# Two transformer blocks, the fp32 down projections: residual kept in SBUF, weight blocks in a ring of four instead of eight

## What is computed

```python
x = x + rms_norm(mix @ w_out[l], post_mix_norm[l])
h = rms_norm(x, pre_ffn_norm[l])
u = causal_dwconv(h @ w_up[l], conv_w[l], conv_b[l])
gate, up = jnp.split(u, 2, axis=-1)
y = (jax.nn.gelu(gate, approximate=True) * up) @ w_down[l]
x = x + rms_norm(y, post_ffn_norm[l])
```

## Time and profile before

| | |
|---|---|
| median of the runs | 2494.13 us (2492.53 to 2497.15) |
| profiled execution, its own time | 2492.89 us |
| its span | 2491.1 us |
| down1 in it, from the first raw block's issue to the last product | about 911.8 to 1155.8 us |
| down2 in it, likewise | about 2235.4 to 2480 us |

### The profile page before, as it was taken

The page is one execution under the profiler, slowest core; times in us unless marked ns, Lnnn a source line. Parts: engine busy times, 40 slices in busy tenths (PEclk is TensorE's granted clock), DMA queues, the critical chain, the costliest instruction groups (busy, mean ns, idle before and its releaser), DMA issues.

```text
span 2491.1 us, 38756 instructions
## 1 busy us (share of the span) xinstructions
PE 2474.5 (99%) x15321; PEld 2133.2 (86%) x15321; DVE 1820.7 (73%) x2218; ACT 1353.0 (54%) x1792; POOL 177.2 (7%) x82
## 2 busy tenths in 40 slices
PE   9999999999999999999999999999999999999998
PEld 9999988888888888888888888888888888888886
DVE  6665675777777779787495968775767777778887
ACT  6554564655555556555545454554555555555554
POOL 1000000030211300000000000000012121120000
PEclk9999999999999999999999999999999999999999
DMA  7765335655566565655655555545666555656664
GB/s 238 256 203 160 119 133 190 215 189 188 189 187 193 187 223 198 221 198 195 191 178 162 177 154 177 154 151 186 204 194 192 187 188 186 195 189 220 220 212 159
DMA packets 242886, 470.75 MB, mean 189 GB/s; under 512 B 14520, under 2 KB 24049, under 8 KB 241601
## 3 DMA queue, kind: packets, MB, share of 16 engines
q1 hardware_dynamic: 240513, 457.64, 56.9%
q0 software_dynamic: 2144, 11.30, 1.4%
q10 hardware_dynamic: 96, 0.02, 0.0%
HBM read 462.59 MB, written 6.32 MB: 188 GB/s over the span
## 4 chain that ended last, share of the span: by engine, by line
PE 96%; DVE 2%; ACT 1%; issue 1%; DMA 0%; SPq 0%; DVEq 0%; ACTq 0%
PE acc L330 13%; PE tp L330 13%; PE acc L310 7%; PE acc L311 7%; PE acc L312 7%; PE tp L332 7%; PE acc L332 7%; PE acc L613 3%; PE acc L612 3%; PE acc L614 3%; PE acc L1382 2%; PE acc L1385 2%; PE acc L1384 2%; PE tp L626 1%; PE tp L627 1%; PE tp L628 1%
## 5 line engine op out<-in xcount | busy, mean ns | idle before, releaser
L297 DVE TENSOR_TENSOR wlo<-raw,whi 128x1024 fp32r<-128x1024 f32 x679 | 847.7, 1256 | 489.3 <-ACT whi L292 487.8
L292 ACT ACTIVATE whi<-raw 128x1024 fp32r<-128x1024 f32 x679 | 716.9, 1059 | 777.4 <-PE acc L332 221.9
L330 PE MATMUL acc<-ahl,whi 128*128 128x512 f32 x1408 | 489.9, 392 | 0.6 <-DVE ahl L415 0.6
L330 PE MATMUL tp<-ahl,whi 128*128 128x512 f32 x1408 | 489.5, 391 | 0.0
L332 PE MATMUL tp<-ahl,wlo 128*128 128x256 f32 x1408 | 394.2, 280 | 0.0
L332 PE MATMUL acc<-ahl,wlo 128*128 128x256 f32 x1408 | 393.9, 280 | 0.0
L330 PEld LDWEIGHTS acc<-ahl,whi 128*128 128x128 f32 x1408 | 263.4, 187 | 58.8 <-issue 1.0
L330 PEld LDWEIGHTS tp<-ahl,whi 128*128 128x128 f32 x1408 | 263.3, 187 | 57.7
L310 PE MATMUL acc<-whi,ahl 128*128 128x512 f32 x752 | 298.7, 397 | 1.9 <-DVE ahl L2209 1.5
L312 PE MATMUL acc<-whi,ahl 128*128 128x512 f32 x752 | 293.0, 390 | 0.0
L311 PE MATMUL acc<-wlo,ahl 128*128 128x512 f32 x752 | 292.7, 389 | 0.0
(11 more groups left out here) (339 smaller groups left out, 3798.4 us busy)
## 6 DMA issues: line engine op xcount, KB each, us to landing
raw<-in_w_up_dram SPq DMA_DIRECT2D x176, 512.0 KB, 4.3
raw<-in_ffn_w_in_dram SPq DMA_DIRECT2D x176, 512.0 KB, 4.3
raw<-in_hgrn_w_in_dram SPq DMA_DIRECT2D x160, 512.0 KB, 3.6
raw<-in_w_in_dram SPq DMA_DIRECT2D x87, 512.0 KB, 3.6
raw<-in_w_down_dram SPq DMA_DIRECT2D x48, 512.0 KB, 5.0
raw<-in_ffn_w_out_dram SPq DMA_DIRECT2D x48, 512.0 KB, 5.2
more<-in_w_down_dram SPq DMA_DIRECT2D x40, 512.0 KB, 5.1
more<-in_ffn_w_out_dram SPq DMA_DIRECT2D x40, 512.0 KB, 4.9
```

Of the source, the lines that this page charges most:

```text
L292: act.activation(whi[:, s, :], raw[:, s, :], ACT.Copy).then_inc(hi_done, 1)
L297: dve.tensor_tensor(wlo[:, s, :], raw[:, s, :], whi[:, s, :].bitcast(F32), ALU.subtract).then_inc(lo_done, 1)
L330: pe.matmul(o[:, ct % 2, :].rearrange("p (a t) -> p a t", a=2), whi[:, s, c], ahl[:, :, kt, :], start=(kt == 0), stop=False, skip_group_ch ...
```

## The change

The residual x has memory of its own all the time (the memory on which `more` lay), `more` is gone, and all 88 blocks of a down projection go through the four places of `raw`. The store of x, the two reads of it and the waits that belong to them are gone.

```diff
-SLOTS = 2 * RING
-SLOT = [m % SLOTS if m < M_DOWN - SLOTS else m % RING for m in range(M_DOWN)]
+SLOT = [m % RING for m in range(M_DOWN)]
 TURN = [SLOT[:m].count(SLOT[m]) for m in range(M_DOWN)]
 BEFORE = [max([k for k in range(m) if SLOT[k] == SLOT[m]], default=None) for m in range(M_DOWN)]
-MAIN_TURNS, MORE_TURNS = SLOT.count(0), SLOT.count(RING)
-LAST_MORE = max(d.n for d in DOWN if d.m is not None and SLOT[d.m] >= RING)
+TURNS_DOWN = SLOT.count(0)
...
-        with ExitStack() as r:
-            x = sb("x", [P, NT, D], where=r)
-        more = sb("more", [P, RING, CK * GC])
+        x = sb("x", [P, NT, D])
...
         def down_slot(m):
 
-            return raw[:, SLOT[m], :] if SLOT[m] < RING else more[:, SLOT[m] - RING, :]
+            return raw[:, SLOT[m], :]
...
-                if m == M_DOWN - RING:
-                    x_back(sp, ph)
                 if m < RING:
                     sp.wait_ge(lo_done, cb[ph] - RING + m + 1)
-                elif m < SLOTS:
-                    sp.wait_ge(sem("x_out"), 16 * (DOWNS.index(ph) + 1))
                 elif BEFORE[m] in SECOND:
                     sp.wait_ge(sem("sums"), ub[ph] + SECOND[BEFORE[m]] + 2)
                 else:
                     sp.wait_ge(lo_done, cb[ph] + FREED[BEFORE[m]] + 1)
...
-        def x_away(pool, b, out_x):
-
-            pool.wait_ge(out_x, 2 * NG)
-            pool.dma_start(x_home(), x[:, :, :]).then_inc(sem("x_out"), 16)
-
-        def x_back(sp, ph):
-
-            sp.wait_ge(lo_done, cb[ph] + LAST_MORE + 1)
-            for t in range(NT):
-                sp.dma_start(x[:, t, :], x_home()[:, t, :]).then_inc(sem("x_back"), 16)
...
             def add(q, t):
                 c = slice(q * GC, (q + 1) * GC)
-                if ph in ub:
-                    dve.wait_ge(sem("x_back"), 16 * NT * (DOWNS.index(ph) + 1))
...
             pool.memset(prime[:, :], 0.0).then_inc(sem(f"{ph}_hid"), 1)
-            x_away(pool, b, out_x)
```

More of the change, by code:

```diff
@@ L260, in bass_two_blocks @@
         tp = [ctx.enter_context(nc.psum_tensor(f"tp{i}", [P, 4, S], F32)) for i in range(2)]
-        landed = [sem(f"landed{i}") for i in range(SLOTS)]
+        landed = [sem(f"landed{i}") for i in range(RING)]
         hi_done, lo_done, chunk_used = sem("hi_done"), sem("lo_done"), sem("chunk_used")
@@ L277, in bass_two_blocks @@
             g += groups
-            m += RING * MAIN_TURNS if name in ub else chunks
+            m += RING * TURNS_DOWN if name in ub else chunks
         def load(sp, n, s, src, kk=CK):
@@ L466, in down_slot @@
         def down_slot(m):
-            return raw[:, SLOT[m], :] if SLOT[m] < RING else more[:, SLOT[m] - RING, :]
+            return raw[:, SLOT[m], :]
         def down_landed(e, ph, m):
-            turns = rb[ph] // RING if SLOT[m] < RING else MORE_TURNS * DOWNS.index(ph)
-            e.wait_ge(landed[SLOT[m]], 16 * (turns + TURN[m] + 1))
+            e.wait_ge(landed[SLOT[m]], 16 * (rb[ph] // RING + TURN[m] + 1))
         def back_load(sp, ph, w):
@@ L491, in back_load @@
                              w_tile(w, CK * (2 * sg + r), i * (2 * GC) + c * GC)).then_inc(landed[SLOT[m]], 16)
-        def x_home():
-            return T["scratch"].rearrange("a p c -> (a p c)")[0:P * NT * D].rearrange("(p n c) -> p n c", p=P, n=NT)
-        def x_away(pool, b, out_x):
-            pool.wait_ge(out_x, 2 * NG)
-            pool.dma_start(x_home(), x[:, :, :]).then_inc(sem("x_out"), 16)
-        def x_back(sp, ph):
-            sp.wait_ge(lo_done, cb[ph] + LAST_MORE + 1)
-            for t in range(NT):
-                sp.dma_start(x[:, t, :], x_home()[:, t, :]).then_inc(sem("x_back"), 16)
         def last_products(pe, ph, k, n, xhi, xlo, kts):
```

## The result

The kernel after takes **2502.87 us**, the median of five runs (2501.91 to 2507.01), against 2492.61 us for the kernel before beside it: a ratio of 1.0035, 95% interval 1.0024 to 1.0047. The profiled executions differ by 10.0 us (spans 2501.1 and 2491.1). The forecast was 2505.3 us, +11.2.

The account below looks back on a forecast made before the run. PE was taken as the bound, busy 2474.5 of 2491.1 us, with loads hidden. Down1 +6.6, down2 +5.4, less 0.8 gained, gave +11.2 on 2494.1: 2505.3 us, range 2496 to 2515.

Parts of the forecast that it names:

- Places 1, 2 and 3: down1's first pair, summed groups at 19, 30, 41: PE 1.2, then 3.4, then 4.6 us late in all.
- The walk through DVE: First pair of down1: late block landings delay DVE's sums, L722 to 970.0, L719 to 989.2 and 1011.1.
- From DVE to PE: Summed steps: a PE step can begin 1.67 us after its low part begins on DVE.
- Place 3: Group at 41: step 44's earliest start 1021.2 against 1016.91, 4.3 us late, 4.7 with b22; 4.6 taken.
- Second pair: Three crossings into summed groups, a loop through b21's landing: 0.6, 0.7 and 0.7 us late, 2.0 us.
- down2: Second down phase: same timeline as down1, quicker landing at place 1 spares 1.2 us, so 5.4 us lost.
- The gain of the tail: Last group of each down phase: without x reads ahead of its blocks, 0.4 us gained per phase, 0.8 in all.
- The blocks land in time: Rival, down phases: landings stay at 4.3 us, no change, +1.4 us, 2495.5 us; chance 0.18.
- It feeds on itself: Rival, down phases: DVE's releases come closer, landings go to 5.5 us for all, +23.8, 2517.9 us; chance 0.15.
- Not slower, but a shade faster: Rival: only the tail changes, with landings under 4 us; 2493.3 us; chance 0.04.
- The ring is not what decides: Rival: another load, at phase start or change of pair, is later still, 5 us per phase, 2515; chance 0.05.
- four signs: Profile after: step 3 PE waits about 12 us; tens of us block waits; last-group waits gone; other phases same to 0.3.

Follow-up runs that it names:

- second profile of the same kernel: The changed kernel run once more, unaltered, beside other kernels on one chip: 2505.59 us, 1.0040 times the kernel before.
- half loads: Changed kernel with each down-projection weight block loaded by half, 256 KB in place of 512 KB: 2493.44 us, 0.9988 times the kernel before.
- five to the last groups: Changed kernel with b22 and b21 used before the two sums and a fifth place for blocks 12 to 51 and 64 to 83: 2495.24 us.
- five, b22 and b21 first: Changed kernel with a fifth place for blocks 12 to 71 and b22 and b21 used before the two sums: 2496.35 us, ratio 1.0010.

## Why the prediction was right, step by step

**What bounds the kernel, and the mechanism: right.** PE does, the loads were hidden, and loads asked for four blocks later reach PE only through DVE in summed groups. The loss ended with shorter landings and with loads six ahead, and stayed with eight places and loads four ahead.

(Places 1, 2 and 3 below are the three numbered points of the prediction's walk, the groups at 19, 30 and 41.)

**The walk through DVE: right to a quarter of a microsecond.** L722 was to move from 968.51 to 970.0, and L719 of the next groups from 985.73 to 989.2 and from 1004.19 to 1011.1. The trace after has 970.22 and 989.38 (the chain above) and, in DVE's timeline, 1011.11:

```profile
1011.11 1.22 DVE L695 TENSOR_TENSOR ybuf<-raw 128x1024 f32<-128x1024 f32 x1 [0.39 <-DMA raw<-in_w_down_dram]
...
1013.39 1.22 DVE L698 TENSOR_TENSOR ybuf<-raw 128x1024 f32<-128x1024 f32 x1
```

**From DVE to PE: the lag was too long.** I had a step begin 1.67 us after its low part begins. In the chain the low part begins at 998.55 and the step at 999.74: 1.19 us, the low part's own 1.15 and 0.04. My 1.67 came from ACT's start less 1.36 us. But ACT starts 0.26 us after the next step has begun (976.12 in the earlier trace rows, 975.86 in PE's timeline), and a step that begins behind a wait takes 0.11 us longer than 1.36. In PE's timeline of the kernel before step 11 begins at 955.33, not at 955.72: the lag in the same rows was 1.28. By luck other errors made this good at places 1 and 2: the low parts came 0.25 us later than walked, PE's own start before was 0.25 us earlier than ACT's (975.86 for 976.12), and the stalled step took its 0.1 us more. Forecast 1.2 and 3.4 in all, measured 1.55 and 3.76.

**Place 3: over-sized.** Forecast 1.2 us more, measured 0.27. L719 came when forecast, but b22, which I had late too, was not: L698 above has no wait. So step 44 began at 1020.34, not at 1021.2, and the late b22 that made 4.3 into 4.6 did not exist. The second profile of the same kernel gave 0.82. The first pair came to 4.03 for 4.6.

**Second pair: the sum near, the block wrong.** I let b21 decide, with 0.6, 0.7 and 0.7 us. In the chain it is b12, for the first sum:

```profile
1078.96 5.58 DMA raw<-in_w_down_dram
1084.63 1.23 DVE ybuf L695
...
1099.51 6.54 DMA raw<-in_w_down_dram
1106.14 1.23 DVE ybuf L695
...
1121.01 5.82 DMA raw<-in_w_down_dram
1126.92 1.23 DVE ybuf L695
```

The sums follow at 21.5 and 20.8 us where PE's period is 20.4, about the 1.03 and 0.51 of the table; the first crossing lost 0.03 inside its margin. Together 1.6, and 2.1 in down2, for a forecast of 2.0. That the size came out with the wrong block was partly luck, though both go out in the same bunch. In the second profile of the same kernel the three crossings lost 0.5, 0.25 and 1.05 us in down1 and 0.35, 0.24 and 0.95 in down2: the sum holds, the single crossings do not.

**down2: right in kind.** I spared it 1.2 us for the quicker landing at place 1. It lost 0.02 there in place of 1.55, and 4.9 us in all without the tail where I had 5.4.

**The gain of the tail: right in kind, too large.** 0.4 us per phase forecast, 0.26 and 0.19 measured in the changed kernel, 0.25 with eight places. PE's wait at L787 was 0.4, but the first matmul of that stretch in the kernel before begins 0.36 us behind the one ahead of it, where 0.23 is the spacing without any wait:

```profile
1146.99 0.39 PE L614 MATMUL acc<-whi,hlo 128*128 128x512 f32 x1
1147.35 0.50 PE L642 MATMUL acc<-whi,hhi 128*128 128x512 f32 x1
1147.69 0.40 PE L643 MATMUL acc<-wlo,hhi 128*128 128x512 f32 x1
```

So 0.13 us ahead of it and 0.11 behind it were lost: the wait listed for the weight load overlaps the matmuls still running.

**The sum.** By phase 6.2 and 5.0 us were forecast, with the tail, and 5.35 and 4.71 came. The errors in down1 are +0.4 at places 1 and 2, -0.9 at place 3, -0.4 at the crossings and +0.1 in the tail; in down2 -0.6 in the first pair, +0.1 at the crossings and +0.2 in the tail. In the median the forecast is 2.4 us high: 0.9 from the sum (the medians are 10.3 apart), 1.5 from the starting median of 2494.1, which is 2492.6 over five runs.

**The rivals.** "The blocks land in time" is refuted by the ten new waits of PE, and half loads show what it would have looked like. "It feeds on itself" would have cost 12 us per phase: DVE did stay late, but the landings did not go to 5.5 for all; their median stayed at 4.8 and 4.5. "Not slower, but a shade faster" needed landings under 4 us, and what it would have gained is what eight places without the traffic show, 0.5 us. "The ring is not what decides" is refuted too: outside the groups of the table no load that came late cost PE anything.

**What I had said would show it.** Three of four signs came: the waits for blocks went from 13 us to 110 on ACT and 10 on DVE, no ACT wait over 5 us at the last group (2.37 was the longest there), and the other phases were the same within 0.2 us. The first pair lost more than the second in both phases (4.03 and 1.57 us in down1, 2.76 and 2.14 in down2), and no loss lay outside the two. The fourth was mis-stated: I wanted 12 us of listed PE waits, and the list has 6.6 for a loss of 10.5 (10.06 and the tail's 0.45). A stalled step costs 0.9 us and is listed with 0.6. Nor did each summed group wait: the groups at 41, 75 and 97 of down1 and those at 19 and 86 of down2 have no wait of PE in the list. And the waits are not all at step 3: at the group at 30 steps 1, 2 and 3 each begin 0.3 to 0.9 late, because DVE needs 2.27 us for a low part and a sum where PE needs 1.36. Once the margin is used, each such step costs the difference, 0.91.

## What to carry to other kernels

Before buffers are taken from a ring, ask how far ahead of need each load then goes out, in microseconds at the pace of the fastest stretch and not at the mean pace; here 4 blocks at 1.36 us, 5.4 us, were too few against landings of 5 to 6 us with DVE's and ACT's work on the block behind them, and 6 blocks, 8.2 us, were enough. If fewer places are a must, first look for an order of work that gives a place back sooner: here it took away more than half of the loss and added no work. If a place is borrowed, look at when it is first free: a load that waits for it holds up all loads behind it in the queue. And price two savings on the same queue together, in all four combinations: a transfer that hides behind a deep ring for 0.25 us can cost 6 us behind a shallow one.

## What the runs showed of the hardware beyond that

**A PE pause costs more than its length.** With the ring of four and x read, PE was idle for about 4 us, and matmuls then started 0.42 us apart in place of 0.23 for some 3 us (granted clock 0.57 as the mean of 4 us, so for the most part at the lower of its two levels, 1.2 GHz, not 2.4), before it was back at 1.00. That cost 1.6 us on top of the pause. (The Trainium skill, "TensorE: Matmul & The Clock Gate", section "HAM oscillation — how this bites in real kernels", tells of waits for DMA that put the array back to the lower clock; the trace agrees for this pause.) The waits of 0.6 us in the changed kernel left the clock at 1.00 throughout down1.

**A phase that ran 2% slower at full clock.** In the profiled execution of "five to the last groups" the first up phase, whose code is the same, ran slower than in the kernel before. The window 600 to 700 of the kernel before and then of that one:

```profile
600.00:700.00 100.00, 100.00 (x579) 88.19 (x578) 74.08 (x90) 54.22 (x67) 19.31 (x6) 1.00 0.60 190
```
```profile
600.00:700.00 100.00, 100.00 (x568) 86.74 (x567) 80.17 (x90) 53.07 (x66) 16.85 (x6) 1.00 0.62 187
```

Eleven matmuls of 579 fewer, the clock at 1.00, DVE busy 80.2 us for the same 90 operations in place of 74.1. The profiled execution of "five, b22 and b21 first" shows the like in the second up phase. These two executions are 11.5 and 8.3 us over their kernels' medians. Other kernels with a median near 2495 us, the one before included, have single runs near 2505 too; no profile shows whether those are of the same kind. The cause was not looked for and stays open; it is why a kernel was judged here by its median and by the two down phases, never by one span.
